# Second mixer: cross scores for the upper half, an update in two column halves, one masked 128x128 operand for the values

## The chip, the cores and the metric

One NeuronCore of a Trainium2 chip runs the whole program in one launch. The metric is the device time in microseconds (us), the median of several executions. The engines are TensorE (PE; PEld are its weight loads), VectorE (DVE), ScalarE (ACT), GpSimd (POOL) and SyncE (SP), which issues most DMAs.

## What is computed

Two transformer-like blocks over 1024 tokens of width 1024 in fp32. The second block puts 16 meta tokens in front (1040 tokens) and has a mixer whose branch A is a gated linear recurrence in 8 heads with 128 key and 64 value channels. Cut to what matters:

```python
f = lbf + (1.0 - lbf) * jax.nn.sigmoid(f_logit)     # decay, per head and key channel
k = 1.0 - f
# S_t = diag(f_t) S_{t-1} + k_t v_t^T ;  o_t = S_t^T q_t   (per head, S is 128 x 64)
# in chunks, with a = cumsum(log f):
o_inter = einsum('bhtk,bhkv->bhtv', q * exp(a), S)
scores  = einsum(q_t * exp(a_t - a_s), k_s)         # s <= t only
o = o_inter + einsum('bhts,bhsv->bhtv', scores, v)
S = exp(a_last)[..., None] * S + einsum('bhsk,bhsv->bhkv', k * exp(a_last - a), v)
```

Beside it the block projects its input to 44 column blocks of 128 (gates, queries, decays, values and so on).

## The kernel before

The second mixer (`mixer2`) runs the recurrence on transposed data: channels on partitions, tokens along the free axis. A head's 1040 tokens are eight full tiles of 128 tokens and one of 16. Two full tiles make a unit; a head has four units (the last one with the 16-token tile), eight heads make 32 slots.

**Scores without overflow.** Inside a tile, `exp(a_t - a_s)` is not formed for all pairs. Pairs within 64 tokens are split into level 0 (the diagonal) and levels 1 to 6 (pairs whose two tokens lie in neighbouring blocks of 1, 2, ... 32 tokens); each level has its own scaled queries and keys `z` (DVE, L3791, from exponentials of ACT, L3598, of distances of POOL, L3477 and L3478). Pairs across the two halves of a tile (64 tokens each) are one more level, the cross level. `scores` computes seven levels for each half (L3991, 14 products that write PSUM partitions 0 to 63 and 64 to 127 in turn, 64 columns each) and the cross level for all 128 keys (L3995, 128 partitions of output). `sc` is 128 x 8 x 64.

**Masks.** `mask` multiplies `sc` by 0/1 masks (L3805; the cross mask is 1 for the keys of the upper half, partitions 0 to 63, and 0 for the others) into `mk`, and one reduce adds the seven levels of each half into `own` (L3809, 128 partitions, 448 columns to 64).

**Outputs.** `outputs` forms a tile's result (64 value channels x 128 tokens, in PSUM) in four products: values of the upper 64 tokens by `own` into the upper columns (L4022), the same values by the cross scores into the lower columns (L4024), the state `S` by the decayed queries over all columns (L4028; not in a head's first tile, where S is zero), and values of the lower 64 tokens by `own` into the lower columns (L4033). The last waits on the semaphore `upper_ready` of the ones before, and the state's update (L4043, keys of a tile by its values, 128 partitions of output) stands between them. Odd heads write partitions 64 to 127 of the output, even heads 0 to 63. DVE turns the update into the next state (`state`, L3818 and L3821).

**The order** is written by hand. In each slot PE runs: a dense piece (24 products of up to 348 columns, L3936), outputs of the second tile of the unit before, scores of this unit's first tile, the keys' transposition (L3976), a dense piece, scores of the second tile, outputs of the first tile, a dense piece (a fourth one in three slots). DVE runs for the next unit the decay (L3767 to L3772), the scan (L3777), queries (L3784), level 1, then the state, level 2, mask and reduce of this unit's first tile, levels 3 and 4, mask and reduce of its second tile, the state, levels 5 and 6 and the last keys (L3796). ACT evacuates the dense pieces (L3530 and L3560), takes logarithm and exponentials (L3589, L3593, L3598, L3605), and once a head activates the whole head's queries and decays (L3567 and L3569).

## Time and profile before

| | |
|---|---|
| Median of 3 runs | 2996.99 us (2994.65 to 2998.09) |
| Profiled execution, span | 3001.8 us |
| PE busy in it | 2922.9 us (97%) |
| DVE busy | 1986.5 us (66%) |
| ACT, POOL busy | 1204.8 us, 1216.1 us |
| Second mixer's recurrence | 1484 to 2085 us |

The page gives each engine's busy time and the costliest groups of instructions. The timeline lists instructions with their start and duration in us, equal neighbours merged (x2, x24), and in brackets how long the engine sat idle before and what ended that. Matmuls are pipelined and their ends are modelled, so a product's cost is read from the start of one to the start of the next, not from its duration.

### The profile page before, as it was taken

The numbers are of one execution on the slowest core, as the hardware profiler recorded it, in microseconds if no ns is written. First come the engines' busy times: TensorE is split into PE (matmuls) and PEld (weight loads), VectorE is DVE, ScalarE is ACT, GpSimd is POOL, SyncE is SP. The second block draws the span as 40 slices with busy tenths as digits, with TensorE's granted clock in tenths as the row PEclk, the third lists the DMA queues.
The fourth block names the chain that finished last, engine by engine and source line by source line (L and its number), as shares of the span: only waits on it lengthen the run. The fifth ranks groups of instructions, "written<-read, shape, count | busy, mean of one in ns | idle before, by whom it ended". The sixth has DMA issues, their size and how long they took to land. (4 is left out here: it accounts for less than half of the span.)

```text
span 3001.8 us, 55447 instructions
## 1 busy us (share of the span) xinstructions
PE 2922.9 (97%) x21780; PEld 2521.5 (84%) x21780; DVE 1986.5 (66%) x2687; ACT 1204.8 (40%) x1872; POOL 1216.1 (41%) x1033
## 2 busy tenths in 40 slices
PE   7999999999999999999999999999999999999998
PEld 6787889787888888778999999898978788888887
DVE  6898765568777777776365656564435766666665
ACT  3232543433333333353465565653433333333233
POOL 0002422327565656531343434342232655555552
PEclk9999999999999999999999999999999999999999
DMA  3111000311111112132111111111440121212112
GB/s 126 49 45 36 3 3 25 127 57 56 53 52 50 55 45 59 42 122 91 43 44 51 36 43 29 44 46 62 149 142 22 53 60 45 59 45 59 46 46 85
DMA packets 205491, 173.25 MB, mean 58 GB/s; under 512 B 10590, under 2 KB 182198, under 8 KB 204918
## 3 DMA queue, kind: packets, MB, share of 16 engines
q1 hardware_dynamic: 198389, 162.02, 17.5%
q10 hardware_dynamic: 6912, 8.52, 0.8%
q8 instruction: 142, 2.33, 0.3%
q14 instruction: 48, 0.39, 0.0%
HBM read 149.41 MB, written 21.10 MB: 57 GB/s over the span
## 5 line engine op out<-in xcount | busy, mean ns | idle before, releaser
L3936 PE MATMUL mix_e<-blk_hi,mix_w_hi 128*128 128x348 f32 (+3 forms) x1056 | 346.8, 328 | 1.5 <-DVE blk_lo L3046 1.2
L3091 DVE TENSOR_TENSOR tokens_x<-ffn_acc,tokens_x 128x512 f32<-128x512 f32 x450 | 302.1, 687 | 67.1 <-PE ffn_acc L2647 67.0
L3936 PE MATMUL mix_e<-blk_lo,mix_w_hi 128*128 128x348 f32 (+3 forms) x1056 | 339.9, 322 | 0.0
L3936 PE MATMUL mix_e<-blk_hi,mix_w_lo 128*128 128x348 f32 (+3 forms) x1056 | 338.9, 321 | 0.0
L2630 PE MATMUL ffn_out<-ffn_T,ffn_w12h 128*128 128x512 f32 x1008 | 311.7, 390 | 4.4 <-POOL ffn_w12l L2508 2.2
L2647 PE MATMUL ffn_acc<-blk_hi,ffn_hid_hi 128*128 128x512 f32 x900 | 309.7, 393 | 2.9 <-issue 2.9
L2508 POOL TENSOR_TENSOR ffn_w03l<-ffn_r,ffn_w03h 128x512 fp32r<-128x512 f32 x126 | 193.5, 1535 | 122.2 <-ACT ffn_w03h L2859 118.5
L2630 PEld LDWEIGHTS ffn_out<-ffn_T,ffn_w12h 128*128 128x128 f32 x1008 | 187.7, 188 | 44.0 <-POOL ffn_w12l L2508 2.9
L3462 POOL TENSOR_TENSOR mix_w_lo<-mix_raw,mix_w_hi 128x1024 fp32r<-128x1024 f32 x44 | 107.1, 2435 | 280.7 <-ACT mix_w_hi L3514 280.5
L2508 POOL TENSOR_TENSOR ffn_w12l<-ffn_r,ffn_w12h 128x512 fp32r<-128x512 f32 x114 | 167.0, 1474 | 108.2 <-ACT ffn_w12h L2859 106.3
L3936 PEld LDWEIGHTS mix_e<-blk_hi,mix_w_hi 128*128 128x128 f32 x1056 | 199.2, 189 | 6.0 <-DVE blk_lo L3046 1.4
L2647 PEld LDWEIGHTS ffn_acc<-blk_hi,ffn_hid_hi 128*128 128x128 f32 x900 | 169.3, 188 | 39.4 <-issue 3.3
L3936 PEld LDWEIGHTS mix_e<-blk_lo,mix_w_hi 128*128 128x128 f32 x1056 | 199.2, 189 | 0.3
L3936 PEld LDWEIGHTS mix_e<-blk_hi,mix_w_lo 128*128 128x128 f32 x1056 | 199.0, 188 | 0.0
L2630 PE MATMUL ffn_out<-ffn_T,ffn_w12l 128*128 128x512 f32 x504 | 196.7, 390 | 0.0
L2647 PE MATMUL ffn_acc<-blk_hi,ffn_hid_lo 128*128 128x512 f32 x450 | 175.7, 390 | 0.0
L3477 POOL TENSOR_TENSOR mix_work<-mix_sf 128x128 f32<-128x128 f32 (+1 forms) x192 | 85.3, 444 | 209.3 <-DVE mix_sf L3777 181.0
L609 DVE SCALAR_TENSOR_TENSOR mixed_conv<-in_c,top_table,mixed_conv 128x1024 f32<-128x1024 f32 x120 | 155.9, 1299 | 3.8
L2859 ACT ACTIVATE ffn_w12h<-ffn_r 128x512 fp32r<-128x512 f32 x124 | 75.3, 624 | 202.6 <-PE ffn_out L2630 197.0
L2859 ACT ACTIVATE ffn_w03h<-ffn_r 128x512 fp32r<-128x512 f32 x122 | 76.5, 629 | 162.6 <-PE ffn_out L2630 105.5
L2508 POOL TENSOR_TENSOR ffn_w12l<-ffn_S,ffn_w12h 128x512 fp32r<-128x512 f32 x42 | 58.0, 1380 | 202.1 <-ACT ffn_w12h L2859 202.1
L2630 PE MATMUL ffn_out<-blk_hi,ffn_w03h 128*128 128x258 f32 (+1 forms) x504 | 134.4, 321 | 2.8 <-POOL ffn_w03l L2508 1.0
(533 smaller groups left out, 7482.2 us busy)
## 6 DMA issues: line engine op xcount, KB each, us to landing
ffn_r<-ffn_up SPq DMA_DIRECT2D x88, 256.0 KB, 3.0
mix_raw<-w_in SPq DMA_DIRECT2D x44, 512.0 KB, 3.8
ffn_r<-w_up SPq DMA_DIRECT2D x88, 256.0 KB, 3.0
ffn_room<-ffn_down SPq DMA_DIRECT2D x20, 512.0 KB, 4.0
ffn_room<-w_down SPq DMA_DIRECT2D x20, 512.0 KB, 4.0
proj_w_raw<-w_in_first SPq DMA_DIRECT2D x19, 512.0 KB, 3.8
branch_gates<-proj SPq DMA_DIRECT2D x16, 520.0 KB, 4.6
wout_raw<-w_out SPq DMA_DIRECT2D x16, 512.0 KB, 3.9
```

Source lines behind the costliest of these rows:

```text
L609: nc.vector.scalar_tensor_tensor(conv[:, f, :], c[:, f, t:t + T], table[:, column:column + 1], conv[:, f, :], ALU.mult, ALU.add).then_inc( ...
L2508: G.by(tt(slots[slot_][1], raw, slots[slot_][0], ALU.subtract), f"lo_{name}")
L2630: mm = nc.tensor.matmul(o, a[:, k, :], rhs, start=fresh and k == 0 and part == 0, stop=k == half - 1 and part == 2, skip_group_check=True)
L2647: mm = nc.tensor.matmul(accs[t % len(accs)], a[:, par, i * P:(i + 1) * P], b[:, h, :], start=part == 0, stop=part == 2)
L2859: A.by(activation(slots[slot_][0], raw, ACT.Copy), f"hi_{name}")
L3091: return vec.tensor_tensor(dst, accs[t % len(accs)], dst, ALU.add)
L3462: tt(w_lo[n % 2][:], raw[:], w_hi[n % 2][:], ALU.subtract).then_inc(lo_ready, 1)
L3477: tt(d4[:, :, 0, :], ref, a4[:, :, 0, :], ALU.subtract)
L3936: last = nc.tensor.matmul(dst[:, 0:m], a[n % 2][:, kd, :], b[:, kd, c:c + m], start=kd == 0 and part_ == 0, stop=kd == KD - 1 and part_ == 2)
```

## The change

The score tile, the masks and `mk` get the cross level in front instead of at the end: index 0 is the cross level, 1 to 7 are the levels of a half. `own` goes away; `mk` has nine slots. The mask product writes slots 1 to 8, then two reduces, one for each 64 partitions, write slot 0 of the upper partitions and slot 1 of the lower ones. So `mk[:, 0:2]` is a 128 x 128 operand: upper keys by (own, cross), lower keys by (0, own), with a block of zeros that is set once before the loop.

The cross scores are computed for the 64 upper keys only (64 x 64). The three value products of a full tile become one of 128 columns over all 128 tokens. The update is computed in two halves of 64 key channels, one into each 64 partitions: the half in the partitions that the output does not use comes before the state product, the other after it. `upper_ready` and its wait go away. The 16-token tile keeps its two products.

```diff
-                vec.tensor_tensor(mk[g % 2][0:n, 0:lv, 0:m], src[:, 0:lv, 0:m], masks[0:n, 0:lv, 0:m], ALU.mult).then_inc(
-                    masked, 1)
+                at = slice(8 - lv, 8) if i < FULL2 else slice(1, 1 + lv)
+                vec.tensor_tensor(mk[g % 2][0:n, 1 + at.start:1 + at.stop, 0:m], src[:, at, 0:m], masks[0:n, at, 0:m],
+                                  ALU.mult).then_inc(masked, 1)
                 dve.wait_ge(masked, g + 1)
                 lv = min(lv, 7)
-                vec.tensor_reduce(own[0:n, g % 2, 0:m], mk[g % 2][0:n, 0:lv, 0:m].rearrange("p l b -> p b l"), AX.X,
-                                  ALU.add).then_inc(added, 1)
+                for x in range(2 if i < FULL2 else 1):
+                    rows = slice(C1 * x, C1 * x + C1) if i < FULL2 else slice(0, n)
+                    last = vec.tensor_reduce(mk[g % 2][rows, x, 0:m], mk[g % 2][rows, 2:2 + lv, 0:m].rearrange(
+                        "p l b -> p b l"), AX.X, ALU.add)
+                last.then_inc(added, 1)
...
-            vec.memset(masks[0:C1, 7, :], 1.0)
-            vec.memset(masks[C1:P, 7, :], 0.0)
+            vec.memset(masks[0:C1, 0, :], 1.0)
+            vec.memset(masks[C1:P, 0, :], 0.0)
...
+            vec.memset(sc[:, :, 0:C1], 0.0)
+            for part_ in mk:
+                vec.memset(part_[C1:P, 0, :], 0.0)
...
-                    last = mm(sc[:, g % 2, 7 * C1:8 * C1], zz, zz[:, C1:P], start=True, stop=True,
+                    last = mm(sc[0:C1, g % 2, 0:C1], zz[:, 0:C1], zz[:, C1:P], start=True, stop=True,
                               skip_group_check=True)
...
-                upper, lower_ = slice(0, C1), slice(C1, P)
-                mm(out[hp, u % 2, c:c + C1], vt[upper, i, hp], own[upper, g % 2, :], start=first, stop=False,
-                   skip_group_check=True)
-                last = mm(out[hp, u % 2, c + C1:c + P], vt[upper, i, hp], mk[g % 2][upper, 7, :], start=False, stop=False,
-                          skip_group_check=True)
+                last = mm(out[hp, u % 2, c:c + P], vt[:, i, hp], mk[g % 2][:, 0:2, :].rearrange("p a b -> p (a b)"),
+                          start=first, stop=not i, skip_group_check=True)
+                if not i:
+                    last.then_inc(out_ready, 1)
+                update(u, i, 1 - h % 2)
                 if i:
-                    pe.wait_ge(state_ready, h * FULL2 + i)
-                    last = mm(out[hp, u % 2, c:c + P], S[:, i % 2, :], qa[:, u % 3, c:c + P], start=False, stop=False,
-                              skip_group_check=True)
-                last.then_inc(upper_ready, 1)
-                update(u, i)
-                pe.wait_ge(upper_ready, h * FULL2 + i + 1)
-                mm(out[hp, u % 2, c + C1:c + P], vt[lower_, i, hp], own[lower_, g % 2, :], start=False, stop=True,
-                   skip_group_check=True).then_inc(out_ready, 1)
+                    mm(out[hp, u % 2, c:c + P], S[:, i % 2, :], qa[:, u % 3, c:c + P], start=False, stop=True,
+                       skip_group_check=True).then_inc(out_ready, 1)
+                update(u, i, h % 2).then_inc(upd_ready, 1)
...
-                mm(upd[:, 0:N], kt[:, u % 2, i % 2, :], vt[:, i, hp], start=True, stop=True).then_inc(upd_ready, 1)
+                return mm(upd[keys_, 0:N], kt[:, u % 2, i % 2, keys_], vt[:, i, hp], start=True, stop=True,
+                          skip_group_check=True)
```

On PE, between a dense piece and the next, outputs of a unit's second tile (of a head's odd tile), scores of the next unit's first tile and its keys. `mix_out` is the result in PSUM, `mix_upd` the update, `mix_sc` the scores; the last figures are output partitions x columns. Before:

```order
L4022 MATMUL mix_out<-mix_work,mix_vt 64x64
L4024 MATMUL mix_out<-mix_work,mix_vt 64x64
L4028 MATMUL mix_out<-mix_work,mix_S 64x128
L4043 MATMUL mix_upd<-mix_vt,mix_kt 128x64
L4033 MATMUL mix_out<-mix_work,mix_vt 64x64
L3991 MATMUL mix_sc<-mix_q,mix_work 64x64 x2
L3991 MATMUL mix_sc<-mix_work 64x64 x12
L3995 MATMUL mix_sc<-mix_work 128x64
L3976 MATMUL mix_e<-top_ident,mix_work 128x128 x2
```

Now, the same place on PE:

```order
L4028 MATMUL mix_out<-mix_work,mix_vt 64x128
L4045 MATMUL mix_upd<-mix_vt,mix_kt 64x64
L4034 MATMUL mix_out<-mix_work,mix_S 64x128
L4045 MATMUL mix_upd<-mix_vt,mix_kt 64x64
L3998 MATMUL mix_sc<-mix_q,mix_work 64x64 x2
L3998 MATMUL mix_sc<-mix_work 64x64 x12
L4002 MATMUL mix_sc<-mix_work 64x64
L3982 MATMUL mix_e<-top_ident,mix_work 128x128 x2
```

Three value products are one, the update is two products around the state product, and no output but the keys' is wider than 64 partitions.

On DVE, a unit's two masks with the levels of the next unit between them (`mix_work` holds `z`, the distances and `mk`), in a head's first unit. Before:

```order
L3805 TENSOR_TENSOR mix_work<-mix_sc,mix_masks 128x512
L3809 TENSOR_REDUCE mix_work<-mix_work 128x64
L3791 TENSOR_TENSOR mix_work<-mix_work 128x16x8
L3791 TENSOR_TENSOR mix_work<-mix_q,mix_work 128x16x8
L3791 TENSOR_TENSOR mix_work<-mix_work 128x8x16
L3791 TENSOR_TENSOR mix_work<-mix_q,mix_work 128x8x16
L3805 TENSOR_TENSOR mix_work<-mix_sc,mix_masks 128x512
L3809 TENSOR_REDUCE mix_work<-mix_work 128x64
L3821 COPY mix_S<-mix_upd 128x64
```

Now:

```order
L3805 TENSOR_TENSOR mix_work<-mix_sc,mix_masks 128x512
L3811 TENSOR_REDUCE mix_work<-mix_work 64x64
L3811 TENSOR_REDUCE mix_work<-mix_work 64x64
L3790 TENSOR_TENSOR mix_work<-mix_work 128x16x8
L3790 TENSOR_TENSOR mix_work<-mix_q,mix_work 128x16x8
L3790 TENSOR_TENSOR mix_work<-mix_work 128x8x16
L3790 TENSOR_TENSOR mix_work<-mix_q,mix_work 128x8x16
L3805 TENSOR_TENSOR mix_work<-mix_sc,mix_masks 128x512
L3811 TENSOR_REDUCE mix_work<-mix_work 64x64
L3811 TENSOR_REDUCE mix_work<-mix_work 64x64
L3824 COPY mix_S<-mix_upd 128x64
```

Each reduce became two on half the partitions; nothing else on DVE moved.

## Rows read from the trace of the kernel before

**Rows 1.** Windows, mixer stretch: length; busy us of PE, PEld, DVE, ACT, POOL; clock, DMA

```profile
1484.00:2085.00 601.00, 597.82 (x5305) 547.15 (x5304) 363.83 (x815) 341.02 (x627) 238.75 (x406) 1.00 0.14 44
```

**Rows 2.** Waits, 1484 to 2085 us: total us, times, longest

```profile
DVE mix_sf L3777 <- ACT mix_work L3589: 79.4, 28, 8.6
...
DVE mix_work L3805 <- PE mix_sc L3995: 45.4, 29, 3.6
...
DVE mix_work L3805 <- PE mix_sc L3991: 18.3, 8, 3.8
...
PE mix_out L4022 <- DVE mix_work L3809: 0.8, 2, 0.5
```

**Rows 3.** Timeline, PE, behind the mixer: start, duration, instruction, [idle before]

```profile
2101.72 0.63 PE L4180 MATMUL branch_out<-branch_obhi,branch_w_hi 128*128 128x348 f32 x1 [4.26 <-PEq L192]
```

**Rows 4.** Timeline, PE and PEld, outputs and scores up to the next dense piece

```profile
1818.51 0.32 PE L4022 MATMUL mix_out<-mix_work,mix_vt 64*64 64x64 f32 x2
...
1818.67 0.28 PE L4024 MATMUL mix_out<-mix_work,mix_vt 64*64 64x64 f32 x2
...
1818.88 0.43 PE L4028 MATMUL mix_out<-mix_work,mix_S 128*64 128x128 f32 x2
...
1819.24 0.43 PE L4043 MATMUL mix_upd<-mix_vt,mix_kt 128*128 128x64 f32 x2
...
1819.61 0.33 PE L4033 MATMUL mix_out<-mix_work,mix_vt 64*64 64x64 f32 x2
...
1819.86 0.34 PE L3991 MATMUL mix_sc<-mix_q,mix_work 128*64 128x64 f32 x4
...
1820.83 0.43 PE L3995 MATMUL mix_sc<-mix_work 128*128 128x64 f32 x2
...
1820.99 0.26 PEld L3976 LDWEIGHTS mix_e<-top_ident,mix_work 128*128 128x128 f32 x2
...
1821.22 0.19 PEld L3936 LDWEIGHTS mix_e<-blk_hi,mix_w_hi 128*128 128x128 f32 x1
```

**Rows 5.** Timeline, PE, scores and outputs of a unit's other place

```profile
1807.37 0.34 PE L3991 MATMUL mix_sc<-mix_q,mix_work 128*64 128x64 f32 x4
...
1808.70 0.32 PE L4022 MATMUL mix_out<-mix_work,mix_vt 64*64 64x64 f32 x2
...
1810.05 0.37 PE L4058 MATMUL mix_e<-mix_inv,mix_expand 16*128 16x130 f32 x1
```

**Rows 6.** Timeline, single instructions: second pass of L4024, second pass of L4028

```profile
1818.73 0.22 PE L4024 MATMUL mix_out<-mix_work,mix_vt 64*64 64x64 f32 x1
...
1819.04 0.27 PE L4028 MATMUL mix_out<-mix_work,mix_S 128*64 128x128 f32 x1
```

**Rows 7.** Line L3040, DVE: count, duration ns min/median/max, first and last start

```profile
L3040 DVE SCALAR_TENSOR_TENSOR ffn_y<-tokens_x,ffn_inv,ffn_gains x8: 1283/1285/1286, 1329.6 to 1373.0; 128x1024 f32<-128x1024 f32 x8
L3040 DVE SCALAR_TENSOR_TENSOR ffn_meta<-ffn_meta,ffn_inv,ffn_gains x1: 1273/1273/1273, 1313.7 to 1313.7; 16x1024 f32<-16x1024 f32 x1
```

**Rows 8.** Timeline, DVE: the two reduces of one unit, what follows the first

```profile
1803.30 0.97 DVE L3809 TENSOR_REDUCE mix_work<-mix_work 128x64 f32<-128x448 f32 x1
1804.18 0.28 DVE L3791 TENSOR_TENSOR mix_work<-mix_work 128x128 f32<-128x128 f32 x1
...
1811.50 0.97 DVE L3809 TENSOR_REDUCE mix_work<-mix_work 128x64 f32<-128x448 f32 x1
```

**Rows 9.** Timeline, all engines, a unit whose chain hangs on ACT

```profile
1606.66 0.46 ACT L3530 ACTIVATE mix_ev<-mix_e 128x348 f32<-128x348 f32 x1 [4.52 <-PE mix_e L3936]
...
1615.57 0.97 DVE L3809 TENSOR_REDUCE mix_work<-mix_work 128x64 f32<-128x448 f32 x1
...
1618.38 0.33 PE L4022 MATMUL mix_out<-mix_work,mix_vt 64*64 64x64 f32 x2
```

**Rows 10.** Timeline, all engines, a unit behind a head's activation

```profile
1895.97 2.28 DVE L3791 TENSOR_TENSOR mix_work<-mix_work 128x136 f32<-128x136 f32 x1 [0.93 <-ACT mix_work L3598]
...
1900.49 0.30 PE L4022 MATMUL mix_out<-mix_work,mix_vt 64*64 64x64 f32 x2 [0.53 <-DVE mix_work L3809]
```

More of the change, by code:

```diff
@@ L3348, in mixer2 @@
         z = [carve(LEVELS2, wide) for _ in range(2)]
-        mk = [carve(8, C1) for _ in range(2)]
-        own = carve(2, C1)
+        mk = [carve(9, C1) for _ in range(2)]
         at[0] = 0
@@ L3371, in mixer2 @@
             s.sem(n) for n in ("d_ready", "el_ready", "z_ready", "elast_ready", "kl_ready"))
-        sc_ready, masked, added, upper_ready, out_ready, upd_ready, state_ready, o_ready = (
-            s.sem(n) for n in ("sc_ready", "masked", "added", "upper_ready", "out_ready", "upd_ready", "state_ready", "o_ready"))
+        sc_ready, masked, added, out_ready, upd_ready, state_ready, o_ready = (
+            s.sem(n) for n in ("sc_ready", "masked", "added", "out_ready", "upd_ready", "state_ready", "o_ready"))
         squared, inv_ready, scaled, finished = (s.sem(n) for n in ("squared", "inv_ready", "scaled", "finished"))
@@ L3445, in sync @@
                     sp.dma_start(w_pool[:], ins["w_pool_2"][0].rearrange("g c d -> c g d")).then_inc(consts_landed, 16)
-                    sp.dma_start(masks[:, 0, :], const_of(consts, "eye")).then_inc(consts_landed, 16)
-                    sp.dma_start(masks[:, 1:7, :].rearrange("p a b -> p (a b)"), const_of(consts, "levels")).then_inc(
+                    sp.dma_start(masks[:, 1, :], const_of(consts, "eye")).then_inc(consts_landed, 16)
+                    sp.dma_start(masks[:, 2:8, :].rearrange("p a b -> p (a b)"), const_of(consts, "levels")).then_inc(
                         consts_landed, 16)
@@ L3990, in scores @@
                     for own_ in parts:
-                        last = mm(sc[own_, g % 2, l * C1:l * C1 + own_.stop - own_.start], lhs[:, own_], rhs[:, own_],
+                        c = (l + 1) * C1
+                        last = mm(sc[own_, g % 2, c:c + own_.stop - own_.start], lhs[:, own_], rhs[:, own_],
                                   start=True, stop=True, skip_group_check=True)
@@ L4015, in outputs @@
                     pe.wait_ge(state_ready, h * FULL2 + i)
-                    mm(out[hp, u % 2, c:c + n], vt[0:n, i, hp], own[0:n, g % 2, 0:n], start=False, stop=False,
+                    mm(out[hp, u % 2, c:c + n], vt[0:n, i, hp], mk[g % 2][0:n, 0, 0:n], start=False, stop=False,
                        skip_group_check=True)
@@ L4020, in outputs, with update @@
                     return
-                upper, lower_ = slice(0, C1), slice(C1, P)
-                mm(out[hp, u % 2, c:c + C1], vt[upper, i, hp], own[upper, g % 2, :], start=first, stop=False,
-                   skip_group_check=True)
-                last = mm(out[hp, u % 2, c + C1:c + P], vt[upper, i, hp], mk[g % 2][upper, 7, :], start=False, stop=False,
-                          skip_group_check=True)
-                if i:
-                    pe.wait_ge(state_ready, h * FULL2 + i)
-                    last = mm(out[hp, u % 2, c:c + P], S[:, i % 2, :], qa[:, u % 3, c:c + P], start=False, stop=False,
-                              skip_group_check=True)
-                last.then_inc(upper_ready, 1)
-                update(u, i)
-                pe.wait_ge(upper_ready, h * FULL2 + i + 1)
-                mm(out[hp, u % 2, c + C1:c + P], vt[lower_, i, hp], own[lower_, g % 2, :], start=False, stop=True,
-                   skip_group_check=True).then_inc(out_ready, 1)
-            def update(u, i):
+                last = mm(out[hp, u % 2, c:c + P], vt[:, i, hp], mk[g % 2][:, 0:2, :].rearrange("p a b -> p (a b)"),
[3 more added lines that the diff above has]
+                update(u, i, 1 - h % 2)
+                if i:
+                    mm(out[hp, u % 2, c:c + P], S[:, i % 2, :], qa[:, u % 3, c:c + P], start=False, stop=True,
+                       skip_group_check=True).then_inc(out_ready, 1)
+                update(u, i, h % 2).then_inc(upd_ready, 1)
+            def update(u, i, half):
                 h = u // UNITS
                 n = h * FULL2 + i
-                hp = slice(64 * (h % 2), 64 * (h % 2) + 64)
+                hp, keys_ = (slice(64 * x, 64 * x + 64) for x in (h % 2, half))
                 await_taken(pe, "kt", u)
```

## The prediction

> **What bounds the kernel now.** The page shows TensorE as by far the busiest engine, so I went to the stretch in which the second mixer runs its recurrence (1484 to 2085 us). Its window: PE busy 597.8 of 601 us, DVE 363.8, ACT 341.0, PE's granted clock at the full 2.4 GHz [rows 1]. Its waits: PE waited for DVE's reduce twice, 0.8 us together, while DVE waited for PE's scores 37 times (45.4 + 18.3 us) and 28 times for ACT's logarithm (79.4 us) [rows 2]. So PE sets the pace there, and time taken out of PE's queue comes off the end as long as DVE and ACT keep up. After the stretch PE waits once, 4.26 us [rows 3], for a chain that starts at its own last products; that shifts with it.
>
> **PE's queue around one tile.** An fp32 product is two instructions (x2 in a row). The steps from start to start [rows 4] are 0.16 us (L4022), 0.21 (L4024), 0.36 (L4028), 0.37 (L4043) and 0.25 (L4033), together 1.35, and in the other tile of a unit the same 1.35, 1808.70 to 1810.05 [rows 5]. Single starts tell what they are made of [rows 6]: one 64-column pass of L4024 takes 0.06 (1818.67 to 1818.73), but from its last pass to L4028 it is 0.15, so 0.09 is lost where the shape of the operand in the array changes (64*64 to 128*64). L4028's passes start 0.16 apart, and the second is 0.20 before the next shape: 0.11 for a pass of 128 columns, 0.05 for a weight load that nothing hides. Shapes change between all neighbours but L4022 and L4024. The scores keep one shape and alternate between the two column halves of the array: 14 products in 0.97 us with one load and one change, 0.83 net, so 0.06 each, where a product alone on its half takes two passes, 0.12.
>
> **What the change gives on PE.** All of a full tile's products get the shape of the scores, 128*64.
> - The three value products become one of 128 columns (0.22); the state product stays (0.22). The update becomes two products of 64 columns: the one in the free column half runs beside the value product, the other costs 0.12. With one load this is 0.61 for 1.35.
> - Outputs, scores, keys (1818.51 to 1821.22, 2.71 us [rows 4]) become 0.61 + 0.83 + 0.12 for the cross product + 0.09 for the change to the keys + 0.23 for the keys (1820.99 to 1821.22) + 0.10 for their load, hidden so far (my estimate: twice the half-wide 0.05) = 1.98. Saved 0.73.
> - Scores, outputs (1807.37 to 1810.05, 2.68 us [rows 5]) become 0.05 + 0.83 + 0.12 + 0.56 + 0.09 = 1.65. Saved 1.03.
> - 32 units of two full tiles: 32 x 1.76 = 56. The eight first tiles of a head have no state product and save 0.14 less each: **55 us**. The 16-token tiles keep their two products.
> - Bounds: no row shows a single product beside a longer one. If the free half's update ran alone it would cost 0.12 x 64 = 8 us (47 left); if the cross product and the last update each shared their time with a product of the other half, 0.12 less per tile, 8 more (63). I take 55, because the score rows show two halves at work at once.
>
> A rule of the Trainium skill speaks against the last point: TensorE: Matmul & The Clock Gate, Part 3 (Packing small matmuls), says that a weight load overlaps a running matmul only when their row groups differ, and these products use all rows. The score rows disagree: 28 instructions with their loads take 0.97 us [rows 4]. What the rule would make of the time is the fourth rival.
>
> **What it costs on DVE.** The reduce becomes two, each over 64 partitions. The trace has no such operation; the nearest rows are one on 16 partitions of 1273 ns where the same on 128 takes 1285 [rows 7]: a half is as long as the whole. The bounds are nothing and a full reduce; I take the full one, 0.88 us from start to start (1803.30 to 1804.18 [rows 8]). 64 x 0.88 = 56 us more, DVE busy 420 of some 560 us. The mask product keeps its 512 columns and the three memsets lie before the loop: nothing. On DVE levels 3 and 4 stand behind the second reduce of a unit's first tile, the state and levels 5 and 6 behind that of the second.
>
> **Where PE would meet that.** I compared the end of the reduce with the start of L4022 in all 64 tiles. A unit's second tile is early by 6 to 11 us (1812.47 against 1818.51 [rows 4, 8]): no loss. Its first tile is early by 2.1 to 7.8 us in 18 of 32 units (1804.27 against 1808.70 [rows 5, 8]). In the others DVE comes late because its chain hangs on ACT: ACT evacuates a dense piece at 1606.66 after 4.52 us of waiting for PE, then come logarithm, scan and levels, the reduce ends at 1616.54, and PE starts at 1618.38, 1.84 us later [rows 9]. That chain gets 0.88 longer (the reduce of the tile before lies in the wait for PE) and PE's way beside it 1.0 shorter (0.73, the cross product and a change of shape): 1.9 us of slack go. Eleven such units have 0.55 to 1.84; what they lack adds up to 7.6 us.
> Three units have 0.26 to 0.30 us, one of them 1900.23 to 1900.49, where PE idles 0.53 already [rows 10]. Just before them ACT activates a whole head, and its chain starts at DVE's first reduce of the unit before, not at a piece of PE. Two reduces and a whole unit's saving on PE count: 0.88 x 2 + 1.76 = 3.5 us, so 3.2 lost each, 9.6. Together **17 us lost**, between 0 and the 42 of the first rival.
>
> **Sum.** 55 - 17 = 38 us. The profiled span is 3001.8, 4.8 us above the median of 2997.0; I take the 38 from both: 2963.8 and **2959**.
>
> **Rivals.**
> 1. DVE's loop takes over. If every unit, not three, hung on DVE's own previous reduce, each would lose 3.5 us less its slack: over the 22 units below 3.5 that is 42 us, gain 13, 2984. For it: after the change the two are nearly even. Against it: in 29 of 32 units the second mask starts within 0.4 us of PE's scores, so the chain is caught up once a unit, and the 79.4 us for the logarithm [rows 2] are largely a wait for PE's pieces, through ACT.
> 2. No loss: ACT and DVE slide forward with PE's earlier pieces; gain 55, 2942. For it: ACT waits for PE in [rows 9]; against it: the slacks of 0.26.
> 3. Slower. DVE's lag is carried from unit to unit: 3.5 x 32 = 112 us against the 64 us in which it waits for PE [rows 2] loses 48; and its reduces are stretched beside POOL's split of the weights, as a multiplication was at 1895.97, 2.28 us [rows 10]. If one in four of the 128 gained 1.7 us, 54, the sum is 55 - 48 - 54 = -47: 3044. It turns slower once the stretch passes 7 us. Against it: the reduces shown take 0.97 [rows 8, 9].
> 4. Weight loads that nothing hides, seven of a tile's eight: 7 x 0.05 x 64 = 22 us of the gain gone, 2981. This is what the skill's rule would do.
> That the change does nothing on PE is ruled out by the order: five products in four shapes become four in one.
>
> **How the numbers follow.** Forecast (2945 to 2974) 0.62; rival 1 0.16; rival 2 0.12; rival 3 0.05; rival 4 0.03; an unforeseen loss that ends near no change 0.02. The range 2942 to 2986 takes in the forecast, rival 4 and most of rivals 1 and 2 and leaves out some 0.15. About 0.2%, 6 us, is what a measurement of this kernel can tell from no change. Faster by more: 0.62 + 0.12 + 0.03 + 0.13 of rival 1 = 0.90. Within: 0.05 (0.03 of rival 1, 0.02). Slower: 0.05.
>
> **What the profile after would show.** From the value product to the next scores 0.6 us instead of 1.35, and no step of 0.15 lost between the value product, the update's halves and the state product; the cross product within 0.12; two reduces of about 0.9 us. The stretch shrinks from 601 to about 563 us. If the step from the value product to the state product is 0.3 or more, the free half is not free. PE's waits for the reduce appear by name, some 14 of them, the longest about 3 us behind a head's activation; if they sum to over 30 us, rival 1 holds; if a halved reduce takes 0.5, rival 2 is nearly right.

## The result

The changed kernel takes 2978.67 us, median of four runs (2970.44 to 2984.15), against 2996.05 us for the kernel before beside it (four runs, 2994.65 to 2998.09): a ratio of 0.9944, 95% interval 0.9926 to 0.9962. That is 17 us less, not 38. A second measurement, `after_again` below, gives 0.9938 (0.9919 to 0.9958), again 17 us. The time lies inside the range on record, and the sign is the forecast's, but more than half of the gain that was forecast is missing.

The profiled execution has a span of 2968.7 us, 33 below that of before, which looks like the forecast. It isn't: the profile of before (3001.8) is of an execution slower than all four runs beside it, and this one is of the fastest of its four. Inside the mixer (first scores to last outputs, 592.7 us before, 569.4 after) the two profiles differ by 23.3 us; 6.5 us lie ahead of it and 3 behind, where the change has no instruction.

The window of the mixer after, with busy us of PE, PEld, DVE, ACT and POOL, PE's granted clock, DMA share and GB/s, answers to [rows 1]:

```profile
1478.00:2058.00 580.00, 545.48 (x5194) 516.77 (x5193) 429.13 (x879) 341.46 (x629) 236.94 (x406) 0.99 0.15 46
```

PE was busy for all but 3 us of that stretch; now 34.5 us are missing, DVE has gone from 363.8 to 429.1 us, and the clock is no longer 1.00. The waits of the same stretch (total us, times, longest) answer to [rows 2]:

```profile
DVE mix_sf L3776 <- ACT mix_work L3588: 48.4, 24, 6.5
...
PE mix_out L4028 <- DVE mix_work L3811: 26.8, 15, 4.0
...
DVE mix_work L3805 <- PE mix_sc L4002: 14.9, 8, 4.2
...
PE mix_out L4023 <- DVE mix_S L3821: 5.2, 4, 1.6
...
DVE mix_work L3805 <- PE mix_sc L3998: 2.8, 6, 1.8
```

DVE's waits for PE's scores have shrunk from 63.7 us to 17.7, and PE's for DVE's reduce have grown from 0.8 to 26.8 (27.9 in 16 waits with one that the view puts down otherwise). In a good part of the units it is now PE that waits for DVE.

**PE's queue.** Outputs, scores and keys of one unit, PE's timeline (start, duration, instruction), which answers to [rows 4]:

```profile
1511.46 0.32 PE L4028 MATMUL mix_out<-mix_work,mix_vt 128*64 128x128 f32 x1
1511.46 0.33 PE L4045 MATMUL mix_upd<-mix_vt,mix_kt 128*64 128x64 f32 x2
1511.62 0.27 PE L4028 MATMUL mix_out<-mix_work,mix_vt 128*64 128x128 f32 x1
1511.72 0.38 PE L4034 MATMUL mix_out<-mix_work,mix_S 128*64 128x128 f32 x2
1511.94 0.22 PE L4045 MATMUL mix_upd<-mix_vt,mix_kt 128*64 128x64 f32 x1
1511.95 0.27 PE L3998 MATMUL mix_sc<-mix_q,mix_work 128*64 128x64 f32 x1
1512.00 0.22 PE L4045 MATMUL mix_upd<-mix_vt,mix_kt 128*64 128x64 f32 x1
...
1512.87 0.28 PE L4002 MATMUL mix_sc<-mix_work 128*64 128x64 f32 x2
1513.09 0.44 PE L3982 MATMUL mix_e<-top_ident,mix_work 128*128 128x128 f32 x2
1513.28 0.41 PE L3942 MATMUL mix_e<-blk_hi,mix_w_hi 128*128 128x348 f32 x1
```

The first update starts with the value product (1511.46 both), so the free column half is free. The second update starts at 1511.94 and the next tile's first score at 1511.95: they too run side by side, each in its half. From value product to scores it is 0.49 us, where 0.61 was forecast. From value product to the first dense product it is 1.82 (1511.46 to 1513.28), in part of the other units 1.71, where 2.71 stood before ([rows 4]) and 1.98 was forecast.

**A unit that waits.** All engines behind a head's activation (unit 22 of units 0 to 31, the one of [rows 10]), each row with the idle time ahead of it:

```profile
1870.17 2.37 POOL L3461 TENSOR_TENSOR mix_w_lo<-mix_raw,mix_w_hi 128x1024 fp32r<-128x1024 f32 x1 [0.53 <-ACT mix_w_hi L3513]
...
1870.45 2.25 DVE L3790 TENSOR_TENSOR mix_work<-mix_work 128x136 f32<-128x136 f32 x1 [0.92 <-ACT mix_work L3597]
...
1871.77 0.28 PE L4002 MATMUL mix_sc<-mix_work 128*64 128x64 f32 x2
...
1873.04 0.68 DVE L3805 TENSOR_TENSOR mix_work<-mix_sc,mix_masks 128x512 f32<-128x512 f32 x1
...
1873.75 1.83 DVE L3811 TENSOR_REDUCE mix_work<-mix_work 64x64 f32<-64x448 f32 x2
...
1875.83 0.45 PE L4028 MATMUL mix_out<-mix_work,mix_vt 128*64 128x128 f32 x1 [3.78 <-DVE mix_work L3811]
...
1876.07 0.42 PE L4028 MATMUL mix_out<-mix_work,mix_vt 128*64 128x128 f32 x1
...
1876.29 0.64 PE L4034 MATMUL mix_out<-mix_work,mix_S 128*64 128x128 f32 x2
```

PE's scores are done at 1872, DVE is still at the levels of the next unit, and the two halved reduces take 1.83 us where one took 0.97. PE idles 3.78 us, where it idled 0.53 before. And then PE is slower: the passes of one value product are 0.24 apart (0.16 in the block above), and the state product's first pass comes 0.22 behind the last of them (0.10 there). The windows around it (busy us of PE, PEld, DVE, ACT, POOL, then the granted clock) say why:

```profile
1866.00:1871.90 5.90, 5.90 (x83) 5.62 (x79) 3.80 (x6) 4.99 (x10) 4.41 (x7) 1.00 0.11 35
1875.80:1881.10 5.30, 5.27 (x22) 5.18 (x23) 5.18 (x15) 1.00 (x3) 0.81 (x2) 0.50 0.06 21
1881.10:1890.00 8.90, 8.90 (x86) 8.61 (x85) 3.34 (x9) 6.13 (x10) 3.07 (x7) 1.00 0.12 41
```

Behind the wait PE runs at 1.2 GHz for some microseconds, then at 2.4 again. The mixer of the kernel before has no such stretch in its profile.

### The profile page after: what moved, and what is told of

Same layout as the page of the kernel before. It is cut to its first block and busy times, and to the rows that moved or that the text cites. A ratio compares the mean times of both kernels' runs of the same rounds, so it can differ in the third digit from the quotient of the medians.

```text
span 2968.7 us, 55321 instructions
## 1 busy us (share of the span) xinstructions
PE 2861.9 (96%) x21652; PEld 2483.6 (84%) x21652; DVE 2051.9 (69%) x2754; ACT 1204.6 (41%) x1872; POOL 1213.7 (41%) x1033
## 3 DMA queue, kind: packets, MB, share of 16 engines
q1 hardware_dynamic: 198389, 162.02, 17.8%
```

## One account for all kernels

Every kernel below was read in the same way, from its profile: the length of the mixer, the time in it in which PE ran nothing, and the time in it at 1.2 GHz. The kernel before has 592.7, 3.2 and 0, so 589.5 us of work at full speed. A microsecond at 1.2 GHz is taken to do half a microsecond's work (dense products start 0.29 us apart there and 0.16 at 2.4 GHz, in waits_old_products below). What the edit saves on PE itself is then 589.5 - length + idle + half of the time at 1.2 GHz. Medians are beside the kernel before on the same chip.

| kernel | median us | of before | ratio (95%) | mixer | PE idle | at 1.2 GHz | saved on PE |
|---|---|---|---|---|---|---|---|
| the changed kernel | 2978.67 | 2996.05 | 0.9944 (0.9926-0.9962) | 569.4 | 34.5 | 17.1 | 63 |
| after_again (the same) | 2975.84 | 2992.46 | 0.9938 (0.9919-0.9958) | 574.9 | 33.9 | 30.7 | 64 |
| one_reduce | 2955.18 | 2992.46 | 0.9870 (0.9849-0.9891) | 552.9 | 19.3 | 17.1 | 64 |
| two_reduces_old_pe | 3006.93 | 2992.46 | 1.0046 (1.0030-1.0063) | 603.8 | 9.4 | 10.2 | 0 |
| late_outputs | 2962.27 | 2992.46 | 0.9892 (0.9875-0.9909) | 559.9 | 19.1 | 10.2 | 54 |
| copies | 2965.08 | 2990.20 | 0.9913 (0.9897-0.9930) | 561.1 | 24.6 | 20.5 | 63 |
| late_copies | 2955.89 | 2990.20 | 0.9888 (0.9871-0.9904) | 549.6 | 11.4 | 6.8 | 55 |
| whole_update | 2984.40 | 2990.20 | 0.9980 (0.9970-0.9990) | 582.3 | 23.4 | 20.5 | 41 |
| cross_only | 2982.82 | 2990.20 | 0.9972 (0.9962-0.9981) | 582.8 | 6.0 | 0 | 13 |
| waits_old_products | 3028.08 | 2996.86 | 1.0101 (1.0083-1.0119) | 625.9 | 21.9 | 34.1 | 3 |
| late_outputs_old_products | 2994.03 | 2996.86 | 0.9989 (0.9978-0.9999) | 596.8 | 3.7 | 6.8 | 0 |
| early_late_copies | 2947.13 | 2996.86 | 0.9836 (0.9819-0.9852) | 546.8 | 7.7 | 10.2 | 56 |

The last column tests the account: a kernel with the old products must come out at 0, and the three that have them (two_reduces_old_pe, late_outputs_old_products, waits_old_products) give 0, 0 and 3; kernels with the same new products must agree, and give 63 or 64. The account holds within some 3 us. For the changed kernel it reads: 63 saved, 31 lost again to more idle time of PE, 8.5 to the clock, 23 left.

## The experiments

**after_again**: the changed kernel itself, beside the others.

> The changed kernel itself, for its spread. Theory: its runs differ by how often PE's clock falls to half behind the waits in the mixer; the time should fall on a line with the mean granted clock of each run, 0.5 us per us spent at half clock; median 2974 to 2982, spread 10 us or more. Rival: the spread has nothing to do with the clock; equal clocks, unequal times.

2975.84 us, with a spread of 13.9, both as expected. Its mixer is 5.5 us longer than in the first profile with as much idle time, and it has 30.7 us at 1.2 GHz instead of 17.1. The clock thus costs the mixer 8 to 15 us, differently in each execution. Over all ten runs of the changed kernel the time goes with the mean granted clock, if not run by run: 2969.38 and 2971.55 at 0.990 and 0.991, 2979.98, 2983.23 and 2984.15 at 0.986 and 0.987. The kernel before moves with it in the same way, from 2989.64 at 0.995 to 2998.94 at 0.992 and 3003.73 at 0.990. The profiled run here (2974.79) lies 1 us from its median, and its mixer is 17.8 us shorter than that of before, so the 17 us of the medians are the mixer's.

**one_reduce**: is it DVE's second reduce that takes the gain?

```diff
-                for x in range(2 if i < FULL2 else 1):
-                    rows = slice(C1 * x, C1 * x + C1) if i < FULL2 else slice(0, n)
-                    last = vec.tensor_reduce(mk[g % 2][rows, x, 0:m], mk[g % 2][rows, 2:2 + lv, 0:m]...
+                last = vec.tensor_reduce(mk[g % 2][0:n, 0, 0:m], mk[g % 2][0:n, 2:2 + lv, 0:m]...
```

> The changed kernel with one reduce over 128 partitions in place of the two halves (the second write of a tile, the lower half's own scores in slot 1, is left out, so the lower tokens lack them; TensorE's work is word for word that of the changed kernel). Theory: the gap between the 38 us forecast and the 17 us measured is DVE's second reduce, which makes PE wait (28 us before value products, 5 us before the 16-token tiles in the profile after) and lets its clock fall in the mixer. Then this kernel is 45 to 53 us faster than before, 2943 to 2951 us, PE waits for the reduce sum to under 10 us, no half-clock stretch in the mixer, and its runs lie as close together as those of before (3 to 4 us). Rival: PE's saving itself is smaller than the 55 us forecast, or is lost outside the mixer; then this one stays near the changed kernel, 2970 to 2980.

2955.18 us, 20.7 less than the changed kernel beside it: the largest single loss is the second reduce. But 2943 to 2951 was expected, and the waits didn't all go. Its waits and its window:

```profile
DVE mix_sf L3776 <- ACT mix_work L3588: 65.6, 25, 7.3
...
DVE mix_work L3805 <- PE mix_sc L4000: 25.9, 14, 3.8
...
PE mix_out L4026 <- DVE mix_work L3809: 13.3, 8, 2.9
...
1481.00:2046.00 565.00, 545.68 (x5203) 518.07 (x5202) 366.26 (x816) 343.03 (x632) 238.08 (x407) 0.98 0.16 48
```

PE still idles 19.3 us with DVE's work as it was. So 16 us of idle time come from PE's own saving, which brings PE to the reduce sooner, and 15 more from the second reduce.

**two_reduces_old_pe**: the other half of that cross. The kernel before with nothing changed but its reduce, over the old products.

```diff
-                vec.tensor_reduce(own[0:n, g % 2, 0:m], mk[g % 2][0:n, 0:lv, 0:m]...).then_inc(added, 1)
+                for x in range(2 if i < FULL2 else 1):
+                    rows = slice(C1 * x, C1 * x + C1) if i < FULL2 else slice(0, n)
+                    last = vec.tensor_reduce(own[rows, g % 2, 0:m], mk[g % 2][rows, 0:lv, 0:m]...)
+                last.then_inc(added, 1)
```

> The kernel before with its reduce split into two halves of 64 partitions, nothing else: the change's DVE part alone, on the old queue of PE. Theory: the second reduce costs as long as a whole one (0.88 us) and only eats slack, so PE waits in the seven units with less than 0.9 us and in the three behind an activation: 3 to 8 us slower, 2999 to 3004. Rival: the halved reduce is cheap or fully hidden, within 2 us of before.

3006.93 us, 14.5 more than before (ratio 1.0046), where 3 to 8 were expected. The mixer is 11 us longer: 6.2 from idle time, the size that was expected, and 5.1 from 10.2 us at 1.2 GHz, which was not. The profile is of this kernel's fastest run; where its median loses 3 us more than the mixer here, no trace shows. Its reduces, in one line of that source line's view (count, duration ns min/median/max, first and last start, forms):

```profile
L3811 DVE TENSOR_REDUCE mix_work<-mix_work x136: 279/949/980, 1481.5 to 2070.6; 64x64 f32<-64x448 f32 x128, 16x16 f32<-16x80 f32 x8
```

A reduce over 64 partitions takes 949 ns, as long as the 0.97 of one over 128 [rows 8]. Halving the partitions saves nothing.

**copies**: one reduce over 128 partitions into a strip of its own, and two copies of 64x64 that put its halves into the masked operand.

```diff
+                if i < FULL2:
+                    vec.tensor_reduce(own, mk[g % 2][:, 2:2 + lv, :]..., AX.X, ALU.add).then_inc(summed, 1)
+                    dve.wait_ge(summed, (g // TILES2) * FULL2 + i + 1)
+                    for x in range(2):
+                        rows = slice(C1 * x, C1 * x + C1)
+                        last = vec.tensor_copy(mk[g % 2][rows, x, :], own[rows, :])
...
```

> The changed kernel with one reduce over 128 partitions into a buffer of its own and two copies of 64x64 from there in place of the second reduce; same result. Theory: PE's waits follow what DVE does between the scores and the operand. A copy of 64x64 takes some 0.15 us, so 0.3 to 0.4 us instead of 0.88 lie behind the first reduce, and the waits of PE for DVE fall between those with one reduce (19 us in all) and with two (34 us): 24 to 27 us, time 2958 to 2968. Rival: the number of DVE instructions matters, not their length; then no better than the changed kernel, 2970 to 2980.

2965.08 us, ratio 0.9913, and 24.6 us of idle time, both in the expected ranges; a copy takes 0.19 us at the median, not 0.15. DVE's timeline of one tile (start, duration), against the pair of reduces in the changed kernel:

```profile
1816.06 0.93 DVE L3812 TENSOR_REDUCE mix_work<-mix_work 128x64 f32<-128x448 f32 x1
1817.02 0.39 DVE L3817 COPY mix_work<-mix_work 64x64 f32<-64x64 f32 x2
1817.45 0.29 DVE L3792 TENSOR_TENSOR mix_work<-mix_work 128x128 f32<-128x128 f32 x1
```

Reduce and copies take 1.39 us from start to the next start. In the changed kernel the pair of reduces took 1.88 (1818.72 to 1820.60 in another unit), and one reduce alone takes 0.85 (one_reduce, 1813.39 to 1814.24). PE's idle time follows that length: 19.3 us at 0.85, 24.6 at 1.39, 34.5 at 1.88, with the saving on PE at 63 or 64 in all three.

**late_outputs**: the outputs of a unit's first full tile move behind the next dense piece, and DVE's update of the state with them, so that the reduce has one more piece's time. Two reduces stay.

```diff
             for u in range(slots):
...
+                if u:
+                    state(u - 1, before(u)[0])
...
                 mask(u, tiles[1])
-                state(u, tiles[0])
```

(On PE the call outputs(u, tiles[0]) goes from behind the third dense piece to behind the fourth.)

> The changed kernel with the outputs of a unit's first tile behind the third dense piece instead of ahead of it (3.8 us more for the two reduces), and the state that follows from them on DVE moved behind the next unit's decay. Same work. Theory: PE's waits for the reduce (longest 4.0 us) vanish and with them the half clock in the mixer: 50 to 57 us faster than before, 2939 to 2947. Rival: DVE's loop is the limit, not the place of the wait; the waits move to the second tile or to the scores, and the time stays at 2965 to 2980.

2962.27 us, 13.6 less than the changed kernel beside it, and some 20 more than expected. The waits for the reduce are gone but for one; others stand in their place:

```profile
PE mix_out L4026 <- DVE mix_S L3821: 10.6, 7, 1.8
...
PE mix_upd L4048 <- DVE mix_S L3821: 6.4, 8, 2.3
...
PE mix_out L4031 <- DVE mix_work L3811: 0.8, 1, 0.8
```

DVE's state is now what comes late, so its lag is still there, met at another product. And PE saves 9 us less. The outputs now stand alone between dense pieces, and the scores too: one block is 0.70 us and the other 1.07, 1.77 together, where scores and outputs back to back take 1.52 in the changed kernel when nothing waits. The outputs alone, on PE's timeline:

```profile
1505.98 0.32 PE L4031 MATMUL mix_out<-mix_work,mix_vt 128*64 128x128 f32 x1
...
1506.25 0.38 PE L4037 MATMUL mix_out<-mix_work,mix_S 128*64 128x128 f32 x2
1506.47 0.28 PE L4048 MATMUL mix_upd<-mix_vt,mix_kt 128*64 128x64 f32 x2
1506.68 0.43 PE L3945 MATMUL mix_e<-blk_hi,mix_w_hi 128*128 128x348 f32 x1
```

The last update starts at 1506.47 and the dense piece 0.21 later: here no scores share its time, and a change of the operand's shape follows. In 32 units 0.25 us would be 8 us of the 9. But in the changed kernel the 16 blocks behind a wait take 1.81 us without the wait, not 1.52, and gain nothing by staying together, so how the 9 us divide is not shown.

**late_outputs_old_products**: the same move over the old products, with one reduce.

> The kernel before with the outputs of a unit's first full tile one dense piece later and VectorE's update of the state moved with it, as in late_outputs, but with the old products and one reduce. The kernel before waits for only 3 us in the mixer, so later outputs can give at most that. If late_outputs gave back 9 us on TensorE because of where the products stand, this kernel is 5 to 9 us slower than the kernel before (0.2 to 0.3%); if its better time lies in the new place itself and not in the waits that it took away, this kernel is faster than the kernel before by 10 us or more, as late_outputs is against the changed kernel.

2994.03 us, ratio 0.9989 (0.9978 to 0.9999). The expectation of 5 to 9 us more fell: nothing is lost on PE. That fits the shapes: the old products changed the shape between scores and outputs anyway, so a dense piece between them adds no change. The loss in late_outputs goes with the new products; that it is their place next to the scores is argued from the shapes. And the place alone is worth 3 us at most, so late_outputs' gain over the changed kernel lies in waits that it takes away.

**late_copies** joins late_outputs and copies.

> Later outputs of a unit's first tile together with one reduce and two copies. Theory: the waits that the later outputs left (19 us in the mixer, for the state of the tile before) come from DVE's load; with 0.5 us less per tile they fall to about 10 us and the half clock in the mixer to under 10 us: 2950 to 2956. Rival: what is left is ACT's chain and does not move: 2959 to 2965 as with the later outputs alone.

2955.89 us (0.9888), the upper end of what was expected: idle time 11.4 us, 6.8 at 1.2 GHz.

**cross_only** and **whole_update**: which edit gives what on PE. The first is the kernel before with the cross scores for their upper half alone (the rest of their place is set to zero once before the loop), the second is the changed kernel with the update as one product of 128 columns.

```diff
-                    last = mm(sc[:, g % 2, 7 * C1:8 * C1], zz, zz[:, C1:P], start=True, stop=True,
+                    last = mm(sc[0:C1, g % 2, 7 * C1:8 * C1], zz[:, 0:C1], zz[:, C1:P], start=True, stop=True,
...
```

> The kernel before with the cross scores for the upper 64 keys alone, nothing else. Theory: in a unit's second tile and in its first, one product of 128x128 with its shape changes becomes one more product of the scores' shape: 0.05 to 0.15 us saved per tile (the change of shape to the next product stays), 4 to 10 us faster than before, and PE's waits for the reduce hardly grow. Rival: nothing measurable (within 2 us).

> The changed kernel with the update in one piece (128 partitions of output) between the value and the state product. Theory: halving the update is worth two changes of shape per tile plus the halves' overlap: the mixer's stretch is 0.3 to 0.4 us per full tile longer on PE, 20 to 26 us, but PE's waits shrink by a part of it (some 6 to 10 us), so 10 to 18 us slower than the changed kernel. Rival: the halves bring nothing (the free half does not run beside the value product), and it equals the changed kernel within 3 us.

cross_only takes 2982.82 us, 7 less than before (ratio 0.9972), and saves 13 on PE; it has no stretch at 1.2 GHz. whole_update takes 2984.40, 6 less than before and so 11 behind the changed kernel, and saves 41. Both are as expected. By differences, the cross scores give 13 us, the one masked value product 28, the halved update 22, together 63. With DVE left alone, a fifth of the saving gives 7 us, while all of it over two reduces gives 17, and two thirds of it (whole_update) 6.

**waits_old_products**: the clock by itself. No product is new; in six units DVE does five more reduces ahead of the first tile's own, into memory that nobody reads.

```diff
+                if u in (3, 7, 13, 19, 23, 27) and i == tiles_of(u)[0]:
+                    for x in range(5):
+                        vec.tensor_reduce(spare[:, x, :], mk[g % 2][0:n, 0:lv, 0:m]..., AX.X, ALU.add)
```

> The kernel before with five more reduces on VectorE, into memory that nobody reads, ahead of the reduce of the first full tile in six of the 32 units (units 3, 7, 13, 19, 23, 27). Each costs 0.88 us, 4.4 us in all; the slack there in the kernel before is 1.22, 1.84, 2.39, 0.30, 0.62 and 0.88 us, so TensorE is made to wait for 3.2, 2.6, 2.0, 4.1, 3.8 and 3.5 us, 19 us together. If the waits alone cost time, the kernel gets 19 us longer and its mixer keeps the full clock. If TensorE's clock falls to half behind such waits, the records show half clock within some us of most of the six, and at 1.7 us or more for each the kernel gets 27 to 32 us longer, though no product of it is new.

3028.08 us, 31 more than before: the 27 to 32 of the clock theory, not the 19 of the waits alone. The idle time is 18.7 us more, as computed, and 34 us of the mixer ran at 1.2 GHz. One of the six, PE's timeline behind the wait, and windows ahead of it, behind it and further on (the last three columns: granted clock, DMA share, GB/s):

```profile
1856.23 0.44 PE L4027 MATMUL mix_out<-mix_work,mix_vt 64*64 64x64 f32 x2 [4.01 <-DVE mix_work L3814]
...
1859.78 0.49 PE L3941 MATMUL mix_e<-blk_lo,mix_w_hi 128*128 128x348 f32 x1
1860.07 0.49 PE L3941 MATMUL mix_e<-blk_hi,mix_w_lo 128*128 128x348 f32 x1
...
1862.04 0.32 PE L3941 MATMUL mix_e<-blk_lo,mix_w_hi 128*128 128x348 f32 x1
1862.20 0.32 PE L3941 MATMUL mix_e<-blk_hi,mix_w_lo 128*128 128x348 f32 x1
...
1846.00:1852.00 6.00, 6.00 (x76) 5.64 (x71) 4.57 (x10) 5.38 (x12) 4.12 (x10) 1.00 0.01 4
1856.30:1861.60 5.30, 5.30 (x21) 4.62 (x22) 3.33 (x11) 1.00 (x3) 0.94 (x2) 0.50 0.29 82
1861.60:1867.00 5.40, 5.40 (x42) 5.15 (x41) 2.45 (x7) 2.96 (x4) 0.00 (x0) 1.00 0.01 3
```

Dense products start 0.29 us apart at 1.2 GHz and 0.16 at 2.4. All six forced waits (2.0 to 4.0 us) are followed by such a stretch, which begins 1.7 to 4.8 us after the wait began; outside of them the mixer has none. So the wait brings on the slow stretch, whatever the products are. Here a wait for DVE cost its own length and then two thirds as much again (18.7 us of waits, 31 measured; in the profile, this kernel's slowest run, the mixer grew by 33).

**early_late_copies**: late_copies with the first tile's mask and reduce ahead of level 2 of the next unit on DVE.

```diff
-                if more:
-                    level(u + 1, 2)
                 mask(u, tiles[0])
+                if more:
+                    level(u + 1, 2)
```

> late_copies with the first full tile's mask and reduce one step earlier on VectorE, ahead of level 2 of the next unit. Where VectorE is late (its chain hangs on ScalarE's logarithm) the reduce comes 0.8 us earlier; where it is early it waits for TensorE's scores, and the levels behind it come later. late_copies still waits for 11 us in the mixer. If its reduces are the late ones, 3 to 5 us of them go and the time falls from 2956 to 2951; if VectorE's later levels are what the next scores wait for, the time rises above 2960.

2947.13 us (2946.49 to 2948.42), ratio 0.9836, 0.9819 to 0.9852. It leaves out nothing of the computation and is the fastest kernel here, 49.7 us below before and below the 2951 expected. Its window and what is left of PE's waits:

```profile
1478.00:2037.00 559.00, 551.33 (x5204) 517.14 (x5203) 397.09 (x945) 344.31 (x631) 236.14 (x406) 0.99 0.16 48
...
PE mix_out L4034 <- DVE mix_S L3829: 4.0, 3, 1.8
...
PE mix_upd L4056 <- DVE mix_S L3829: 2.2, 1, 2.2
```

Against late_copies 3.7 us of idle time are gone, and the profiled spans differ by 1.5 us (2948.1 and 2946.6). The medians differ by more: the kernel before beside them differs by 6.7 us (2990.20 and 2996.86), and late_copies' profile was its fastest run (2950.16 to 2957.87 in all) and this kernel's its slowest; where late_copies loses time in its other runs, no trace here shows.

## Why the prediction was right and wrong

**TensorE sets the pace, and its time comes off the end: right for the saving, not for what is left of it.** The 63 us are there in the account. What broke is the condition "as long as DVE and ACT keep up": the stretch shrank by 23 us in the profile, where 38 were forecast.

**The saving on PE: 55 forecast, 63 measured; the upper bound was right.** The prediction named the case: the last update shares its time with a product of the other half, 0.12 us. It does (1511.94 beside 1511.95). The keys' load, for which 0.10 was added, costs nothing visible either (L3982 to the dense piece 0.19 us, forecast 0.33). The cross product cost what was assumed, 0.22 with the change of shape (1512.87 to 1513.09), so the other half of the upper bound's reason did not come, and the scores took 0.92 us in this unit for 0.83. The error is 8 us, in the good direction; that it ends on the upper bound of 63 is in part luck. Not foreseen was that behind a wait the block takes 1.81 us without the wait, not 1.52, some 0.3 more in each of 16 units; the 63 has that in it. The fourth rival, loads that nothing hides, is ruled out by the same rows: eight passes of outputs and updates start within 0.54 us (1511.46 to 1512.00). By the rule in the Trainium skill (TensorE: Matmul & The Clock Gate, Part 3) that a load overlaps a running matmul only when their row groups differ, these loads would not overlap, since all products use all row groups; the trace disagrees, and the measurement decides.

**The free column half, the one change of shape: right.** The two updates add 0 between them where scores follow; whole_update prices their split at 22 us.

**The halved reduce as long as a whole: right.** 951 ns at the median of 128 of them; the pair adds 1.03 us for each tile, where 0.88 was taken. DVE's busy time of 429 us was forecast as 420. Here is the line of all of them:

```profile
L3811 DVE TENSOR_REDUCE mix_work<-mix_work x136: 280/951/977, 1484.0 to 2039.4; 64x64 f32<-64x448 f32 x128, 16x16 f32<-16x80 f32 x8
```

**The waits: 17 us forecast, 31 more measured. This is the first step that failed.** The prediction gave each unit its own chain that starts anew at a piece of PE, so that it loses 1.9 us of slack, and let three (2, 19 and 22, behind a head's activation) hang on DVE's work of the unit before and lose 3.5. A unit's slack before and its wait after, from the timelines of both kernels, together say what it lost. PE's idle time above that of the kernel before, in us:

| units | forecast | measured |
|---|---|---|
| 2, 19 and 22, behind a head's activation | 9.6 | 9.9 |
| ten others of the forecast: 1, 3, 5, 6, 7, 23, 26, 28, 29, 30 | 6.6 | 11.5 |
| 11 and 27 | 1.0 | 5.3 |
| 10 | 0 | 0.4 |
| waits of the 16-token tiles' outputs | 0 | 4.2 |
| together | 17 | 31 |

Three things were wrong, about equally. First, the slack lost in an ordinary unit was mis-sized: it was 2.1 to 2.4 us in nine of the ten, not 1.9, since the pair of reduces adds 1.03 us and not 0.88 and PE's way beside it shrinks by 0.9 to 1.0 (2.71 to 1.82 or 1.71) and not by 0.73. Second, units 11 and 27 changed their chain. Both stand behind a head's activation too, but in the kernel before ACT waited for a piece of PE just ahead of it, so they were counted as ordinary (27) or as having enough slack (11). In the changed kernel that wait is gone, and ACT comes to the activation out of DVE's and POOL's work of the unit before. Unit 27, before and after:

```profile
1974.63 0.46 ACT L3560 ACTIVATE mixed_oa<-mix_e 128x348 f32<-128x348 f32 x1 [1.15 <-PE mix_e L3936]
...
1949.67 0.40 POOL L3476 TENSOR_TENSOR mix_work<-mix_sf 128x128 f32<-128x128 f32 x1 [2.11 <-DVE mix_work L3790]
...
1950.52 0.42 ACT L3597 ACTIVATE mix_work<-mix_work 128x256 f32<-128x256 f32 x1 [2.50 <-POOL mix_work L3477]
...
1968.09 0.29 PE L4028 MATMUL mix_out<-mix_work,mix_vt 128*64 128x128 f32 x1 [3.40 <-DVE mix_work L3811]
```

Its slack was 0.88 us and its wait is 3.40, so it lost 4.3, as did unit 11 (2.40 and 1.94); units 2 and 22 lost 4.2 and 4.0, unit 19 3.3. Two pairs of reduces and a whole unit's saving on PE, 2 x 1.03 + 63/32, come to 4.0. Third, the outputs of the 16-token tiles wait for DVE's state behind the same late chain (L4023 in the waits above, 5.2 us in four waits, where two waits of 1.0 us stood before). The prediction had no term for them.

The lateness is not carried on through all units. DVE's slack at the second mask did go: it starts within 0.4 us of PE's scores in 11 of 32 units, where it was 29, and up to 5.6 us late in the others. But DVE still waits for ACT's logarithm 24 times, and ACT ahead of it mostly for a piece of PE, and there the chain starts anew: neighbours that all wait lose the same, 2.37, 2.40 and 2.40 us in units 5 to 7, 2.38, 2.37 and 2.34 in units 28 to 30. So the first rival (every unit hangs on DVE's previous reduce and loses 3.5, 42 us of waits) holds in these five units, perhaps in units 14, 15 and 18 (they lost 3.1 to 3.2 us and had the slack for it), and not in the others, and its sign did not come: PE's waits for the reduce sum to 27.9 us, not to over 30. one_reduce shows that even with DVE untouched 16 us of idle time would have come, from PE's saving alone. The division by units is read from the traces of before and after, and after_again repeats it within 0.1 us in units 11, 22 and 27; no run changes the chain of a unit by itself.

**The clock: not in the sum. This is the second step that failed.** The prediction read 1.00 in [rows 1] and kept it, without a term for what a wait does to it. With waits of 1 to 4 us in it, the mixer loses 8.5 us in the profile and some 15 in after_again. It is the second part of the missing gain, and explains why neither 34.5 us of waits nor the saving of 63 alone gives the result: 63 - 31 - 8.5 = 23 in the profile, and with the heavier clock loss of the other runs 63 - 31 - 15 = 17, which is the median. after_again's profiled run is within 1 us of its median; that the first measurement's median run has the same loss is inferred from its clock, not read in a trace.

**Slower than before (the third rival): no.** Its loss by lag was too high, since the lag is not carried from every unit to the next. DVE operations of levels that take over 1 us, as the one at 1870.45 (2.25 us) beside POOL's split, are 15 in the mixer, where 16 stood before; the longest of the 128 halved reduces took 977 ns.

**What settles it.** The cross of reduces and products: on the old products the second reduce costs 14.5 us, on the new ones 20.7; and PE's idle time falls in step with DVE's length for the tile, 34.5, 24.6, 19.3. What is not settled is how much of each wait is due to which edit in which unit, since the two edits do not add up unit by unit (unit 27 waits 2.48 us with one reduce, 1.28 with two over the old products, 3.40 with both); and how the clock picks its moment: in the profile of the changed kernel a wait of 0.82 us (1758.3) has a slow stretch behind it, and those of 2.98 and 3.40 have none.

## What to carry to other kernels

Before a saving on the bounding engine is booked, roll the loop forward by hand with the new lengths of both engines, unit after unit, and ask in each unit which wait its chain starts from and whether that wait is still there: a slack read from the old trace holds only while its chain starts at the same place. Where the matrix engine runs near full load, price a wait above its own length (here 1.25 to 1.8 times, and 1.0 in cross_only), since its clock may fall behind it. And judge an edit with a cost on a second engine together with the order on that engine: the same products gave 17 us with two reduces in the old place, and 50 with one reduce, two copies and an order that lets them come late.

## What the runs showed of the hardware

- TensorE's granted clock fell from 2.4 to 1.2 GHz for some microseconds behind waits of 0.8 to 4 us in a queue that was otherwise full, and rose again with the queue full. Six forced waits, six stretches; cross_only, with single waits up to 1.2 us and 6 us in all, had none. In all kernels above, each of these stretches in the mixer began within 5 us of the start of a wait of 0.8 us or more.
- Two products in different column halves of the array ran at the same time with all 128 rows in use by both, also where one belonged to an update and the other to the next tile's scores, with their loads hidden.
- A reduce of 448 into 64 took 951 ns on 64 partitions and 930 to 970 on 128; a 64x64 copy 192 ns at the median and 258 on average.
- Taking two blocks of the same operand shape apart cost 0.25 us where neither waits (0.70 and 1.07 for 1.52); taking apart two of different shapes cost nothing that the account shows.
